# Square sums of three head groups as rows of 256 tokens, by ones on 32 columns of the array each

## What is computed

```python
outs = jnp.stack([short_conv_mixer(...), nsa_mixer(...), gla_mixer(...), gmlp_mixer(...)], axis=2)
outs = rms_norm(outs, grp_gain.reshape(N_MIXERS, GROUP_WIDTH))
return outs.reshape(B, S, D_MODEL) @ w_o
```

## Time and profile before

| | |
|---|---|
| median of 3 runs | 1518.88 us |
| the profiled execution | 1518.78 us, its span 1517.1 us |
| PE busy | 1437.3 us, 95% |
| DVE, ACT, POOL busy | 71%, 50%, 27% |
| mean granted TensorE clock | 0.988 of full speed |

### The profile page before, as it was taken

One profiled execution on the slowest core, in us unless ns is written; L12 is line 12 of the kernel. 1 busy time (PEld: TensorE's weight loads), 2 busy tenths in 40 slices (PEclk: granted clock), 3 DMA queues, 4 the chain that ended last, 5 costly groups with the idle time before them and its releaser, 6 DMA issues.

```text
span 1517.1 us, 24648 instructions
## 1 busy us (share of the span) xinstructions
PE 1437.3 (95%) x10229; PEld 1329.3 (88%) x10229; DVE 1084.3 (71%) x1448; ACT 762.5 (50%) x1097; POOL 406.7 (27%) x391
## 2 busy tenths in 40 slices
PE   2899899999999999999998899999999999999998
PEld 2888799977899799977998888999889998799987
DVE  5887797799557697799776567776477667565544
ACT  3556465534656465434875346444364444454432
POOL 0221320398121030397000321101419421220022
PEclk9999899999999999999999999999999999999999
DMA  9783659799352469798342025777557656455650
GB/s 392 278 321 118 236 232 350 290 350 346 112 209 84 165 267 347 286 350 330 139 168 98 1 87 215 287 288 261 194 191 283 218 218 226 172 198 219 223 207 28
DMA packets 49502, 340.71 MB, mean 225 GB/s; under 512 B 6640, under 2 KB 7024, under 8 KB 9072
## 3 DMA queue, kind: packets, MB, share of 16 engines
q1 hardware_dynamic: 46224, 333.04, 58.8%
q10 hardware_dynamic: 3168, 6.10, 1.1%
HBM read 338.04 MB, written 1.08 MB: 224 GB/s over the span
## 4 chain that ended last, share of the span: by engine, by line
PE 74%; DVE 10%; POOL 9%; issue 3%; ACT 3%; DMA 1%; SPq 0%; POOLq 0%; DVEq 0%; ACTq 0%
PE PS L592 48%; PE PS L908 14%; POOL acts_hi_lo L890 5%; POOL acts_hi_lo L892 4%; DVE ring L469 2%; DVE weights_hi_lo L458 1%; DVE X L1033 1%; PE PS L957 1%; PE PS L564 1%; DVE spare L771 1%; DVE arena L1030 1%; PE PS L2508 1%; DVE arena L1032 1%; ACT spare L736 1%; DMA X<-in_x_dram 1%
## 5 line engine op out<-in xcount | busy, mean ns | idle before, releaser
L458 DVE TENSOR_TENSOR weights_hi_lo<-ring,weights_hi_lo 128x1024 fp32r<-128x1024 f32 x426 | 550.5, 1316 | 279.1 <-ACT weights_hi_lo L449 278.0
L449 ACT ACTIVATE weights_hi_lo<-ring 128x1024 fp32r<-128x1024 f32 x426 | 444.7, 1058 | 476.4 <-PE PS L592 272.0
L592 PE MATMUL PS<-hi,weights_hi_lo 128*128 128x256 f32 x3456 | 546.2, 282 | 9.9 <-ACT hi L730 8.3
L592 PEld LDWEIGHTS PS<-hi,weights_hi_lo 128*128 128x128 f32 x3456 | 467.7, 189 | 13.0 <-issue 11.1
L908 PE MATMUL PS<-weights_hi_lo,acts_hi_lo 128*128 128x512 f32 x1584 | 377.6, 399 | 3.6 <-DVE heads L1730 2.0
L908 PEld LDWEIGHTS PS<-weights_hi_lo,acts_hi_lo 128*128 128x128 f32 x1584 | 298.4, 189 | 77.1 <-issue 2.7
L890 POOL CAST acts_hi_lo<-arena 128x256 fp32r<-128x256 f32 x142 | 134.3, 946 | 783.4 <-PE PS L908 436.0
L592 PE MATMUL PS<-lo,weights_hi_lo 128*128 128x256 f32 x1728 | 339.3, 281 | 0.0
L592 PEld LDWEIGHTS PS<-lo,weights_hi_lo 128*128 128x128 f32 x1728 | 263.0, 189 | 0.2 <-DVE lo L777 0.2
L469 DVE CUSTOM_DVE_ANT_0 ring<-ring,cond 128x1024 f32<-128x1024 f32 x192 | 253.2, 1356 | 9.7 <-DMA ring<-in_stream_dram 8.7
L892 POOL TENSOR_TENSOR acts_hi_lo<-arena,acts_hi_lo 128x256 fp32r<-128x256 f32 x142 | 170.1, 1198 | 11.4
(11 more groups left out here) (369 smaller groups left out, 1130.7 us busy)
## 6 DMA issues: line engine op xcount, KB each, us to landing
ring<-in_stream_dram SPq DMA_DIRECT2D x313, 1024.0 KB, 4.9
gate_row<-gate_rows_dram ACTq DMA_DIRECT2D x8, 512.0 KB, 3.6
constS<-in_const_dram SPq DMA_DIRECT2D x1, 1856.0 KB, 8.9
cond<-in_rows_dram SPq DMA_DIRECT2D x2, 512.0 KB, 5.2
X<-in_x_dram ACTq DMA_DIRECT2D x1, 1024.0 KB, 9.9
smallS<-in_small_dram SPq DMA_DIRECT2D x1, 883.0 KB, 8.0
out_dram<-X SPq DMA_DIRECT2D x2, 256.0 KB, 2.0
out_dram<-X ACTq DMA_DIRECT2D x2, 256.0 KB, 2.0
```

Of the source, the lines that this page charges most:

```text
L449: act.activation(wsp[:, g % 2, 0, at:at + HALF], ring[:, n % RING, at:at + HALF], ACT.Copy).then_inc(*ready.one())
L458: dve.tensor_tensor(wsp[:, g % 2, 1, at:at + HALF], ring[:, n % RING, at:at + HALF], wsp[:, g % 2, 0, at:at + HALF].bitcast(F32), ALU.subt ...
L592: mm = pe.matmul(o, lhs, rhs, start=k + g + j == 0, stop=k == KD - 1 and j == 2, skip_group_check=True)
```

## The change

Where `sums` made each group's sums as two columns, `sums_at_once` makes each as a row. The ones are now stationary, 128 rows by 32 columns of them, and the squares of 256 tokens move past; group number i takes columns 32i to 32i+31 of the array and gives 32 equal rows on partitions 32i to 32i+31 of one bank. The six products (three groups, two blocks) replace twelve. The root and the reciprocal then run over 96 partitions of 256 values (`gw`, in the fourth part of `sq`, free until the attention's own squares) where they ran over 128 partitions of 6 values. `spread_row` picks a group's row by a column of the identity, broadcast to 128, against the 96x256 values: one product of 256 columns where two of 128 were. Group 1 keeps `sums` and `spread_group`.

```diff
+            wide = 3
+            gw = sq[0:32 * wide, 3, 0, :]
...
+                def sums_at_once(bank):
+                    for c in range(2):
+                        for i in range(wide):
+                            if c == 0:
+                                pe.wait_ge(*gsq.at(i + 1))
+                            mm = pe.matmul(PS[32 * i:32 * i + 32, bank, 0:SEQ], ones[:, 0:32], sq[:, i, c, :], start=c == 0, stop=c == 1,
+                                           tile_position=(0, 32 * i), skip_group_check=True)
+                    return mm
+
+                def spread_row(i, bank, at, first):
+                    pe.matmul(PS[:, bank, at:at + SEQ], ident[0:32 * wide, 32 * i:32 * i + 1].to_broadcast((32 * wide, P)), gw,
+                              start=first, stop=True, skip_group_check=True).then_inc(*gsp.one())
...
-                for i in range(3):
-                    mm = sums(i, 2, 2 * i, i == 0)
-                mm.then_inc(*gsum.one())
+                sums_at_once(2).then_inc(*gsum.one())
...
-                spread_group(0, 2, 0, True)
-                spread_group(1, 2, 256, False)
+                spread_row(0, 2, 0, True)
+                spread_row(1, 2, 256, False)
...
-                spread_group(2, 2, 0, True)
+                spread_row(2, 2, 0, True)
...
-                act.activation(gr[:, 0:6], PS[:, 2, 0:6], ACT.Sqrt, bias=cst("eps"), scale=1.0 / 256).then_inc(*grt.one())
+                act.activation(gw, PS[0:96, 2, 0:SEQ], ACT.Sqrt, bias=cst("eps")[0:96], scale=1.0 / 256).then_inc(*grt.one())
...
-                dve.reciprocal(gr[:, 0:6], gr[:, 0:6]).then_inc(*grc.one())
+                dve.reciprocal(gw, gw).then_inc(*grc.one())
```

## The result

The changed kernel takes 1524.87 us (median of 11 runs, 1522.19 to 1526.50) against 1518.88 us (11 runs, 1516.03 to 1523.63): a ratio of 1.0033, with a 95% interval of 1.0021 to 1.0044. Timed anew, it was 1522.50 against 1519.00, ratio 1.0013 (1.0002 to 1.0024). The ratios are not the quotients of the medians, which would be 1.0039 and 1.0023. By the ratios it is slower, by some 2 to 5 us. The profiled execution took 1522.99 us, its span 1521.3 us.

What follows compares the result with a forecast made beforehand. PE is in flight 95% of the span, but DVE's work decides when the weight products start; faster sums give 3.3 us at most. Forecast 1518.8 - 0.2 (instructions) + 2.1 (clock) = 1520.7 us, own range 1519 to 1523, overall 1517.0 to 1524.0.

Steps and rivals of the forecast that it cites:

- The sums and the root: PE's sums in 0.9 us and ACT's root in about 0.40 us, both done before DVE reaches the reciprocal.
- The reciprocal: On DVE, 256 values a partition take 1.77 us where 0.19 stood; called the deciding term.
- The spread: On PE, four pieces of 256 columns, some 0.9 us or 1.8 at half clock, covered by DVE's masks and maxima.
- DVE's gain: DVE's waits for the sums, 1.77 and 1.54 us, vanish against the longer reciprocal: -0.3 us first attention, 0 second.
- The clock: PE's new idle gaps leave the clock low when weight products (L908) begin, in one attention or partly both: +2.1 us.
- the slower rival: Both attentions begin weight products at half clock for at least twelve products: +4.2 us, 1522.8, up to 1525; chance 0.13.
- The sum: Whole kernel: 1518.8 - 0.2 by instructions + 2.1 by the clock = 1520.7 us.
- the cheap reciprocal: Rival: DVE's 256 values cost an ordinary pass, 0.35 us; -3.1 us, 1515.7; chance 0.07.
- the holding clock: Rival: PE's clock holds or is back before the weight products; only -0.2 is left, 1518.6; chance 0.25.
- Whether the pieces run side by side: Rival on PE's sums: pieces in a row end at 135.5, still ahead of DVE at 137.0; no time difference.

Runs made afterwards that it cites:

- a short reciprocal: Changed kernel with DVE's reciprocal taken of 6 of the 256 values: weight products start 11.48 us after the first scores in both attentions, against 13.0.
- the filled gaps: Changed kernel plus five products before the spread and four before the weight products, results unused: 1522.21 us against 1520.77 for the kernel before, ratio 1.0007.

## Why the prediction was right, and where it was not

- **The sums and the root** did as written: PE's 12 pieces took 1.39 us with the wait for the third square, ACT's wait was gone, the root took 0.47 us for the 0.40 assumed, and none of it was on the way to the weight products.
- **The reciprocal** was the deciding term and was sized well: 1.77 us from the rows, 1.744 measured. The estimate from the Trainium skill ("VectorE: DVE Perf Modes", First, the fixed hardware budget), 2.3 us from a repeat count of 8, is too long; the slope between the 8-value row and this one is 6.2 ns a value. (Its price was also added up a little low: 0.53 us twice is 1.1 on the sum, not 0.9.) With a short reciprocal the weight products start 1.54 us earlier.
- **The spread** was covered by masks and maxima, as predicted, even in the first attention where it ran at half clock for 2.07 us.
- **DVE's gain** is the step that failed. "-0.2 us or so" is near what the execution that was profiled gives, -0.4 and -0.2, by luck of that execution. The waits of 1.77 and 1.54 us were taken as the kernel's, but they were those of a draw with a low clock in both attentions. In the four profiles of before these starts add up to 23.0 to 26.7 us, with a mean of 25.1, against a steady 26.0. The term's mean is +0.9 us: the reciprocal costs 1.54 us in each attention, 3.1 in all, and the sums give back 2.2 in the mean where 3.3 was taken.
- **The clock** was the right mechanism, in the right place, by the right row, and also sized too small: it was set at 2.1 us for both attentions together, and the streams lost 2.6 in the mean. The forecast had one attention hit in full; in three of four profiles both were, by 0.8 to 1.9 us each. So two hits came, as in the slower rival, but not under its condition: no stream ran twelve pieces at half clock, ten at most, and in the first profile the second attention's stream began at 1.00. The rule of the Trainium skill ("TensorE: Matmul & The Clock Gate", HAM oscillation), that waits between bursts make each burst start cold, agrees with the filled gaps, streams of 5.67 us instead of up to 7.60, but not with every wait here: behind 2.43 us of waiting the stream began and stayed at 1.00.
- **The sum**: the two terms together were forecast at +1.9 and measured at +3.5. 1520.7 was forecast for the median; 1524.87 lies 0.9 above the stated range, while 1.0033 of the 1518.88 before is 1523.9, at its edge, and the second measurement's 1522.50 lies within it. Both terms were too small, and the 2.7 us outside the attentions, most of them the pace of the dense products, had no term at all, so the direction and the two mechanisms are what was right, and the range held only barely.
- **The rivals**: the cheap reciprocal and the holding clock did not come. Whether the pieces run side by side made no difference, as said.

## What to carry to other kernels

A sum that is cheap on PE as a row can be dear behind it: 256 values on each of 96 partitions take the DVE reciprocal 1.74 us, where 6 on each of 128 take 0.19, and DVE's work, with POOL's split behind it, was what the products waited for. Idle gaps that a saving opens ahead of a burst of products have a price of their own when the low clock then falls on the burst: here 2.6 us in two streams, beside the 3.1 that the reciprocal costs. A gap does not bring it down every time, so look at the granted clock where the burst starts. Waits read from one execution depend on the clock that this execution drew, so take a term that rests on such a wait as a range over both levels of the clock.

## What was not expected of the hardware

Products of one kind in one program, fed without a wait, came at three paces, 117.4, 118.7 and 120.1 ns apart (L592, phases of 743 and 1031 pieces), fixed within a phase and different, for most phases, from one execution to the next. On 1031 pieces the ends of that range are 2.8 us apart, which is near the size of the effect studied. What picks the pace stays open.
